# Two neighbours change places: ScalarE's memory piece and its exponentials, VectorE's scaling and its memory piece, in the first mixer's loop over 48 attention items

## The reference, cut to what matters

```python
def _even_mixer(h, w_in, ...):
    aq, ak, av, ao, ai, af, bq, ... = _split(h @ w_in, EVEN_SIZES)
    ya = _mlstm(aq, ak, av, ao, ...)     # the "memory": 4 heads, decayed products of q, k and v
    yb = _nsa(bq, ...)                   # attention: 8 heads, three branches
    return jnp.concatenate([ya, yb], -1) @ w_out

# _nsa, for each block of queries, in each branch:
s = einsum(q, keys);  p = _masked_softmax(s, mask);  o = einsum(p, values)
o = g0 * o_cmp + g1 * o_sel + g2 * o_win
# _mlstm: S = (q k) * exp(decay);  num = S v;  h = num / max(|den|, exp(-m));  layer norm;  times sigmoid(o)
```

## Time and profile before

| | us |
|---|---|
| median of 3 runs | 3416.18 (3413.83 to 3416.23) |
| profiled execution, its own time | 3413.44 |
| its span | 3412.1 |
| the items' loop, by the first and the last of its instructions | about 126 to 358 |
| TensorE busy, of the span | 3250.6 (95%) |
| VectorE, ScalarE, GpSimd busy | 2044.4, 1461.8, 916.4 |

### The profile page before, as it was taken

One profiled execution on the slowest core, in us unless ns is written; L12 is line 12 of the kernel. 1 busy time (PEld: TensorE's weight loads), 2 busy tenths in 40 slices (PEclk: granted clock), 3 DMA queues, 4 the chain that ended last, 5 costly groups with the idle time before them and its releaser, 6 DMA issues.

```text
span 3412.1 us, 47807 instructions
## 1 busy us (share of the span) xinstructions
PE 3250.6 (95%) x20089; PEld 2882.8 (84%) x20092; DVE 2044.4 (60%) x3016; ACT 1461.8 (43%) x2248; POOL 916.4 (27%) x415
## 2 busy tenths in 40 slices
PE   8988999999879999999999999999999999999998
PEld 6876889988567899979999878899899998789998
DVE  6557656453774644568556736665775566367556
ACT  4464345443433544445334323543453343235433
POOL 3210033331511233312233331323222332312232
PEclk9999999999999999999999999999999999999999
DMA  3310323231112233232232323322323323232232
GB/s 131 113 38 1 112 99 112 99 105 56 50 38 78 96 111 100 93 99 86 94 105 87 115 71 99 104 95 93 106 88 104 105 87 112 75 99 98 88 105 75
DMA packets 239814, 308.97 MB, mean 91 GB/s; under 512 B 8336, under 2 KB 168096, under 8 KB 239088
## 3 DMA queue, kind: packets, MB, share of 16 engines
q1 hardware_dynamic: 236016, 291.41, 26.0%
q0 software_dynamic: 3584, 14.52, 1.2%
HBM read 303.80 MB, written 2.10 MB: 90 GB/s over the span
## 4 chain that ended last, share of the span: by engine, by line
PE 75%; DVE 19%; ACT 4%; issue 2%; DMA 0%; POOL 0%; DVEq 0%; ACTq 0%
PE bank L594 24%; PE bank L596 23%; PE bank L595 23%; DVE wlo L2069 3%; ACT whi L1317 1%; DVE wraw L2091 1%; ACT P_e L1641 1%; DVE xl L2142 1%; DVE raw_w L2091 1%; DVE wkk_o L2887 1%; DVE gb L2884 1%; DVE P_e L2566 1%; PE bank L614 1%; PE bank L1256 1%; PE bank L1247 1%
## 5 line engine op out<-in xcount | busy, mean ns | idle before, releaser
L3141 POOL TENSOR_TENSOR wlo<-wraw,whi 128x1024 fp32r<-128x1024 f32 (+3 forms) x219 | 565.3, 2584 | 1586.8 <-ACT whi L1317 1586.3
L594 PE MATMUL bank<-xh,whi 128*128 128x256 f32 (+1 forms) x2456 | 723.6, 295 | 48.9 <-DVE zt L2264 19.9
L1317 ACT ACTIVATE whi<-wraw 128x1024 fp32r<-128x1024 f32 (+3 forms) x426 | 440.6, 1038 | 676.5 <-PE bank L596 547.2
L596 PE MATMUL bank<-xh,wlo 128*128 128x256 f32 (+1 forms) x2456 | 718.7, 293 | 0.0
L595 PE MATMUL bank<-xl,whi 128*128 128x256 f32 (+1 forms) x2456 | 714.7, 291 | 0.0
L594 PEld LDWEIGHTS bank<-xh,whi 128*128 128x128 f32 x2456 | 467.2, 190 | 69.9 <-issue 27.6
L3141 POOL TENSOR_TENSOR wlo<-raw_w,whi 128x1024 fp32r<-128x1024 f32 (+1 forms) x130 | 311.5, 2400 | 723.7 <-ACT whi L1317 723.7
L595 PEld LDWEIGHTS bank<-xl,whi 128*128 128x128 f32 x2456 | 467.2, 190 | 10.2
L596 PEld LDWEIGHTS bank<-xh,wlo 128*128 128x128 f32 x2456 | 466.2, 190 | 10.4
L594 PE MATMUL bank<-whi,uh_w 128*128 128x512 f32 x1216 | 473.9, 390 | 0.0
L596 PE MATMUL bank<-whi,ul_w 128*128 128x512 f32 x1216 | 473.3, 389 | 0.0
(11 more groups left out here) (401 smaller groups left out, 5087.1 us busy)
## 6 DMA issues: line engine op xcount, KB each, us to landing
wraw<-in_w_in SPq DMA_DIRECT2D x26, 1024.0 KB, 5.1
wraw<-in_ffn_w_down SPq DMA_DIRECT2D x20, 1024.0 KB, 5.1
raw_w<-in_ffn_w_down SPq DMA_DIRECT2D x20, 1024.0 KB, 5.1
raw_w<-in_mlp_w SPq DMA_DIRECT2D x19, 1024.0 KB, 5.1
wraw<-in_mlp_w SPq DMA_DIRECT2D x17, 1024.0 KB, 5.2
wraw<-in_ffn_w_gate SPq DMA_DIRECT2D x32, 512.0 KB, 4.7
raw_w<-in_ffn_w_gate SPq DMA_DIRECT2D x32, 512.0 KB, 4.8
raw_w<-in_ffn_w_up SPq DMA_DIRECT2D x32, 512.0 KB, 4.3
```

The source lines that it names most:

```text
L594: M.matmul(o, lh, rh, start=start, stop=False, skip_group_check=more)
L596: return M.matmul(o, ll, rh, start=False, stop=stop, skip_group_check=more)
L1317: A.activation(hi, raw, ACT.Copy).then_inc(*k.w_hi.inc(("hi", j)))
L3141: G.tensor_tensor(lo[:, 0:n], raw[:, 0:n], hi[:, 0:n].bitcast(F), ALU.subtract).then_inc(*k.w_lo.inc(("lo", j)))
```

## The change

On ScalarE the iteration's first memory piece now stands ahead of first(n), the exponentials. On VectorE scaled(n - 1) now stands ahead of the memory piece in all iterations; before, it did so only for items 0 and 1. TensorE, GpSimd and SyncE have the same instructions in the same order as before.

```diff
@@ scalar_program, even()
         for n in range(N + 3):
+            next(units, None)
             if n < N:
                 first(n)
-            next(units, None)
             if n >= 9 and n % 3 == 0:
                 next(units, None)
             if 0 <= n - 2 < N:
@@ vector_program, even()
             if n < N:
                 first(n)
-            if 0 <= n - 1 < 2:
+            if 0 <= n - 1 < N:
                 scaled(n - 1)
             next(units, None)
-            if 2 <= n - 1 < N:
-                scaled(n - 1)
             if n >= 9 and n % 3 == 0:
                 next(units, None)
```

## The result

| | before | after |
|---|---|---|
| median, us | 3415.47 (3413.83 to 3416.23) | 3388.28 (3386.31 to 3388.67) |
| profiled execution, own time and span | 3413.44, 3412.1 | 3388.17, 3386.9 |

The ratio is 0.992, 95% interval 0.9908 to 0.9932. The kernel is 27.2 us faster by the medians and 25.3 by the spans. Forecast were 3401 and at least 3391: the direction was right, the size too small.

The account below looks back on a forecast made before the run. VectorE and ScalarE handing work back and forth in the small memory pieces, with TensorE idling, was taken as the bound. Less 14.5 and 1.4, plus 0.8, makes 15.1 us off the median 3416.2: 3401, range 3391 to 3411.

Parts of the forecast that it names:

- What bounds the loop: Small memory pieces: neither TensorE nor VectorE is full; VectorE waits 26.8 us in all as engines hand work back and forth.
- Rival (c): Rival, 7%: VectorE's round isn't the loop's pace; waits move to TensorE's scores, only two small terms stay, about 3416.
- (b): Rival, 14%: banks that VectorE sets free late decide nearly everything; gain 5.4 us, so 3411.
- a wait removed from VectorE is worth only what TensorE then no longer idles: Small memory pieces: per stretch the smaller of VectorE's waits and TensorE's idle time counts, at most 19.3 us.
- the cut to three quarters: Small memory pieces: TensorE's waits on the scaling counted in full, on banks by half; 14.5 us of 19.3.
- Rival (a): Rival, 14%: banks follow in full, 21.9 us, so 3394; some clock may come back, at most down to 3389.
- The meeting of gates and decays: Behind TensorE's last product of the values: ScalarE's two splits no longer wait for VectorE, 1.4 us earlier, bounds 0 and 3.4.
- The loop's start: Item 0's `PT` copy on ScalarE, for which TensorE waits, comes 0.8 us later; bounds 0 and 2.1.
- The products of the values: Up to 206 TensorE is full, so nothing counted; 4.0 us to an item covers ScalarE's later exponentials.
- Rival (d): Rival, 7%: slower; exponentials need the same iteration's product, ScalarE's tail stands open behind 16 products, 29.6 us, so 3431.
- The table loads: ScalarE loads four tables fewer, 5.1 us together; counted as nothing outside the meeting, since they lie beside full TensorE work.
- the signs announced: Small pieces: VectorE's waits on ScalarE nearly vanish, TensorE's on the scaling falls below 1 us, 136 us shrinks by 14.

Follow-up runs that it names:

- b_pe: Kernel before, with two more overwritten score matmuls in each score product of branches 1 and 2 of items 18 to 39 (56 in all): 3415.59 us.
- a_pe: Changed kernel, with two more overwritten score matmuls in each score product of branches 1 and 2 of items 18 to 39 (56 in all): 3394.0 us.
- copies_act: Changed kernel, with VectorE's `PT` copies of odd items from 17 on given to ScalarE: 3386.33 us.
- a_dve: Changed kernel, with each of VectorE's 44 maxima of items 18 to 39 computed twice: 3405.19 us.
- after_again: The changed kernel, unchanged, measured once more: 3391.56 us.
- dve_only: VectorE's half of the change alone; ScalarE keeps the old order, exponentials ahead of its memory piece: 3392.29 us.
- act_only: ScalarE's half of the change alone; VectorE keeps the old order, scaling behind its memory piece from item 2 on: 3390.82 us.
- act_from16: Changed kernel, but with ScalarE's half only from item 16 on and its old order ahead of that: 3387.71 us.

## Why the forecast had the right sign and too small a size

**What bounds the loop: right.** From item 18 to 42 the question and answer between VectorE and ScalarE is the path before: doubled exponentials cost 21.8 us there, doubled maxima 17.1, and added matmuls 0.8. Rival (c), no change, is out, and so is (b), that banks decide: TensorE's only wait in 214.92 to 248.23 is one of 0.2 us on a `PT` copy, though rows 7 had 3.9 on the scaling, 2.2 on `gb` and 1.5 on `PTe`. The banks came free earlier in full, because the round itself is shorter.

**The failed step: "a wait removed from VectorE is worth only what TensorE then no longer idles", and the cut to three quarters behind it.** From item 16 to 47 the forecast had 14.5 us, and the timelines have 216.57 to 348.93 against 214.92 to 324.43, 132.36 and 109.51: 22.9 us. Of the 8.4 that are missing, 4.8 went with the quarter that was taken off (19.3 less 14.5): the banks, counted by half, came free in full. The other 3.6 lie above the cap of 19.3 itself. For items 18 to 36 the wait was 17.2, TensorE's idle time 72.87 - 60.18 = 12.7, the gain 17.7. The gain is larger than the cap. It is made of two parts: idle time fell from 12.7 to 0.5 us (55.18 - 54.70), and busy time from 60.18 to 54.70 for the same work. So a window's busy time is not the work that stays. Of these 5.5 us at most 3.6 are the clock: 0.95 in both windows before, 1.00 after (35.00 x 0.05 + 37.87 x 0.05). At least 1.8 are something else, and other pairs of windows at clock 1.00 have it too: items 36 to 42 show 20.09 us busy before and 18.99 after, with 121 and 122 matmuls, and items 18 to 27 show 30.53 in `b_pe` and 27.48 in `a_pe`. That matmuls are shown as busy while they wait would fit this, but was not measured by itself.

What the gain is made of shows on VectorE. In items 18 to 36 its waits fell from 17.2 to 1.0 and its busy time from 52.86 to 51.45, together 17.6 of the 17.7 us. From item 16 to 42 the waits on ScalarE were 22.9 us, VectorE still waits 3.5, and its busy time fell from 79.86 to 78.21: together 21.1 of 21.4 (107.45 less 86.01). The right term was VectorE's waits in full.

The Trainium skill, "Perfetto Trace Analysis", section "Identifying the Most-Contended Engine", says that the busy share of matmuls is no good measure of how near TensorE is to its limit, and to take the share of the peak rate that the matmuls reach and the busy share of weight loads instead. The trace agrees with the first: 60.18 and 54.70 us for the same work. The page's reason is that pipelined matmuls look smaller in a trace; here the same work looked larger before. Weight loads are no fixed measure here either: 47.65 us before and 44.59 after. The share of the peak was not worked out.

Why may one take the waits in full, though TensorE was nearly full after? Because here the two limits lie close together by chance: with the waits gone, VectorE is busy 51.45 of 55.18 us and TensorE 54.70. `copies_act` and `a_pe` show that TensorE is in the way now, and `a_dve`, that VectorE has not left the path. Had TensorE had 6 us more to do, some of the gain would have been lost, as `a_pe` lost it.

**Rival (a), 3394 to 3389 at 14%, comes nearest**, and its number is in part luck. The banks followed in full, as it says. The clock rose as well, but `b_pe` shows that in items 18 to 27 this was worth nothing: there the clock is 1.00 and TensorE has more to do, and they take 35.03 us, where before took 35.00 at 0.95. So the clock's fall was beside the path there. What brought the time down to the far end of (a) is that VectorE's waits count in full. The third stretch, which (a) has against itself, has the most idle time only as a share (7.4 of 27.50 us); in us it is the first, with 8.0.

**The meeting of gates and decays, -1.4: about right in these two executions.** By TensorE's own instructions, from the product that starts at 187.02 (187.38 after) to item 18's first score product (221.75 and 220.80), it took 34.73 us and takes 33.42, 1.3 less. The splits no longer wait for the maxima. In the other executions of after's order up to there the same stretch takes 30.89 to 33.32 us, and in those of before's order 35.12 to 35.18, so the gain is 1.3 to 4.3 us. With it goes the clock, 0.75 in after and 1.00 in `a_pe` from the last product's end to item 18's scores (below).

**The loop's start, +0.8: wrong.** TensorE's wait for `PT` fell from 2.20 to 1.49 instead of growing, and a new one of 2.0 us stands ahead of it, at 145.59, on the exponentials. From the loop's first score product to the first product of the values in item 6 it was 33.10 us (126.23 to 159.33) and is 32.36 (127.32 to 159.68), 0.7 less. `after_again` has 32.36 as well, at a clock of 0.95 as in before, so the clock is not the cause; `dve_only` has 33.03 and `act_only` 32.39, so ScalarE's half is. Which wait it took away was not taken apart.

**The products of the values, 0: right.** By VectorE's maxima, items 5 to 12 took 35.34 us and take 33.90, which looks like a gain. But TensorE has 295 matmuls in the first of these windows and 283 in the second: VectorE's maxima have shifted against TensorE's work. From one product's start to that of another six products on it takes 27.69 us in before, with 230 matmuls, and 27.70 in after, with 231:

```profile
159.33:187.02 27.69, 27.48 (x230) 26.92 (x231) 13.47 (x33) 16.33 (x42) 9.18 (x2) 1.00 0.23 77
159.68:187.38 27.70, 27.49 (x231) 26.93 (x231) 13.41 (x38) 15.24 (x43) 9.17 (x2) 1.00 0.23 77
```

The first row is before, the second after. So of the 2.7 us of items 0 to 16 none came there. By TensorE's score products the gain up to item 18 is 2.0 us (95.52 less 93.48), where the forecast had 0.6: 0.7 at the start and 1.3 at the meeting.

**Rival (d), ScalarE's tail behind products**, is real in small: three waits with 6.6 us in all, not at every product. They were no net loss, since `act_from16`, with waits of 6.1 us in their stead, takes the same time.

**The table loads** counted as nothing: nothing here speaks against it, and no run isolated them.

Of the signs announced, VectorE's waits on `PTe` and `den` vanished, the one on `xl` fell from 3.9 to 1.4 us, and ScalarE's exponentials wait 15.1 us for the maxima in the whole loop, where it was 91.9. TensorE's wait on the scaling is gone from items 16 to 42. That its remaining waits would name `PTe` and `gb` was wrong.

## What to carry to other kernels

When two in-order engines ask each other in turn, look for work that needs neither answer and put it between question and answer on either engine; one side is enough for most of it (17.2 us of waits became 3.5 or 2.5), and the two sides don't add up. Price such a wait by its full length, as long as no other engine becomes the limit, and test for the next limit with work added to the engine that seems nearly full: 56 matmuls that cost 0.8 us before and 7.3 after say more than its busy share. Measure a stretch by the starts of the instructions whose pace you ask for: VectorE's maxima showed 1.4 us of gain among the products where TensorE had none. Don't cap a gain by the idle time of a nearly full engine where its clock was below 1.00 or its instructions wait.

## What the runs showed of the hardware

TensorE's granted clock fell behind pauses of only 1.6 to 1.7 us. In before, behind the pause of 1.62 us, and behind one of 1.72 us that ended at 271.05:

```profile
252.00:253.60 1.60, 0.00 (x0) 0.00 (x0) 1.46 (x8) 0.00 (x0) 0.00 (x0) 1.00 0.00 0
253.60:256.00 2.40, 2.20 (x8) 1.60 (x8) 1.50 (x4) 1.35 (x6) 0.00 (x0) 0.68 0.00 0
256.00:258.00 2.00, 2.00 (x13) 2.00 (x12) 1.83 (x8) 0.36 (x2) 0.00 (x0) 0.53 0.00 0
...
271.05:273.00 1.95, 1.95 (x11) 1.95 (x12) 1.03 (x6) 1.28 (x7) 0.00 (x0) 0.62 0.00 0
```

The second and third rows stand behind the first pause; the clock was 1.00 up to its end. It does not fall each time: behind pauses of 1.54 us (to 246.29), 1.72 (to 296.52) and 1.62 (to 309.85) in the same trace it stayed at 1.00. Behind the wait of 3.19 us for item 15's exponentials, which after, `a_pe` and `a_dve` have alike, it was 0.58 in after (215 to 220) and 1.00 in the other two, and items 15 to 18 took 15.15 us in after and 12.63 in both others. So 2.5 us of a single profile can be the clock's, the same order of instructions doesn't always bring the same fall, and what decides it stays open. 1.00 is 2.4 GHz, and 0.53 is nearly all of a stretch at 1.2.

The loop's first maxima started between 132.56 and 133.92 from one execution to another, while the time from item 0 to 16 agreed within 0.1 us among executions of one order. Differences between two starts inside the loop are thus told far more finely than by the whole kernel's time, whose medians for the changed kernel were 3388.28 and 3391.56.
